# Two heads' scores side by side in the row halves of the array, the decay in one pass, and a gate row made earlier

## The chip, the cores and the metric

The kernel runs on one core of one Trainium2 chip, as one program. The metric is device time in microseconds (us), the median of three runs. A lower number is better. Everything is fp32 in and out. TensorE is the engine PE in the rows, VectorE is DVE, ScalarE is ACT, GpSimd is POOL, SyncE is SP.

## What is computed

One sequence of 512 tokens of width 1024 goes through a first block and then two further layers. The parts that the change touches, in short form:

```
# first block, branch a (sparse attention), 8 heads of 64
dots  = einsum('bqhd,bsd->bqhs', qi, ki)            # 8 index heads, ONE shared key
score = einsum('bqhs,bqh->bqs', relu(dots), wi)     # then causal, top 128 keys per query
logits = (qa . ka) * 64**-0.5, on the kept keys     # 8 heads, ONE shared key
# first block, branch b (forgetting attention), 8 heads, own keys
c = cumsum(log_sigmoid(fb + b_forget))              # per head
logits[t,s] = (qb_t . kb_s) * 64**-0.5 + c_t - c_s, causal
# second layer pair, odd layer: neighbourhood attention, 8 heads, own keys
logits = [ (q . k_window) * 64**-0.5 + bias , (q . k_ctx) * 64**-0.5 ]
# odd layer, fourier branch and the end
y = real(fft2(u)); out = (gates * [attention, y]) @ w_out
x = x + gate_row * rmsnorm(out)                     # gate_row: a modulation of the layer
```

The term c_t is the same for all keys of a query and drops out of the softmax. The kernel adds only minus c_s, called the decay.

## The kernel before, in words

**Number format.** Each fp32 operand of a large product is split in a high part (fp32r) and a low part (the rest, also fp32r), and a product is made of three passes: high times high, high times low, low times high. All passes of a product accumulate in one PSUM bank. A bank holds 128 partitions times 512 columns.

**Weights.** A list `STREAM` orders all weight matrices in units of 128 x 512. ACT makes a unit's high part (L1209), POOL its low part (L1043, `low_weights`), PE consumes it (L591, `tiles`). Four units fit (`ROOM = 4`). `high(u)` makes ACT cast up to unit u, and `ahead(chunk)` casts a chunk and the next three units. ACT works strictly in program order, so a wait ahead of such a cast also holds up the weights.

**Attention as a pipeline by hand.** In three stages PE goes through steps s. A step has the scores of a head for 128 queries (one stationary tile, the keys moving), four transposes or fewer of an older step's probabilities, for every second step the values product, and some pieces of a large matrix product that is fed in between (`feed`). The stages are:

- index stage, 24 steps `("i", i)`, heads outside, query tiles t = 1 to 3 inside; the keys are w = 128 (t+1) wide; ACT applies relu (L1339), DVE accumulates (L1950);
- stage ab: 32 steps of branch a, then 32 of branch b, in pairs of heads, w = 128 (t+1), t = 0 to 3. DVE makes the maximum (L2017 or L2022), ACT the exponential (L1379 or L1388), DVE divides (L2033), PE transposes (`turn_both`, L797), ACT and DVE copy, PE makes the values (`values_both`, L811). Scores lie in banks s % 3;
- stage n: 32 steps, keys 512 (bank s % 2) plus 256 of the context (bank 2); lines L975 to L977 scores, L986 transposes (`turn_near`), L999 values, DVE L2342 to L2363, ACT L1716 to L1736. The probabilities lie in three buffers `N_P`.

**Queries before.** A stationary tile always has 128 rows, though a head has 64 features. In the index stage and branch a, where the key is shared and is stored twice, the tile of one head has the high part in one half of the rows and the low part in the other (`STACKED`): two passes, against the high and the low key. In branch b and stage n two heads share a feature tile; the query of one head is made by a mask that zeroes the other's 64 rows: three passes. The masked pairs are prepared per head by ACT (`prep`) and by DVE or POOL (`low_query`, two POOL instructions each in b and n) into the four places of `QM`.

**Decay before.** Branch b adds three more passes per head (`decay`): a stationary tile of 8 rows, the one-hot of the head, against the high decay, the same against the low decay, and identity times causal mask over the 128 columns of the diagonal.

**The values product** writes the two heads of a pair to partitions 0 to 63 and 64 to 127 of one bank, with stationary tiles of 64 columns (`128*64` in the rows).

**The decay itself** is made early (`CT`, one ACT copy L1304 and one DVE subtraction), at a point where ACT's next work is weight casts.

**After the index stage** DVE has 4 rotations, the low keys of b and 16 rounds of top-8 (`L1987`, `L1990`), then gates, and frees PSUM banks for PE as it goes.

**The end of the kernel.** Order on PE: product `ud`, product `dft`, the fourier mix (L1021, L1022), `gate_rows(1)` (L856, two fp32 products of 512 columns, four instructions), products `oo0` and `oo1`. ACT copies the mix, waits for all low parts, issues two row loads (L1782, L1783), waits for DVE to finish the gate row (`act.wait_ge(sig("row1"), 2)`), issues four loads of x, and only then casts the weights of `oo0` beyond the first. DVE makes the gate row (`modulation`, L2052, L2054) when the two row loads are in.

Of the kernel before, what the change touches and what calls it, by code (L numbers as in the profile page):

```python
# [20 lines left out]
F32 = mybir.dt.float32  # L21
# [5 lines left out]
P = 128  # L27
S = 512
# [55 lines left out]
for _name, _w in (("g_pre", 8), ("npre0", 8), ("npre1", 8), ("bmod0", 24), ("bmod1", 24), ("c", 8),  # L84
                  ("c_ctx", 8), ("conv", 12), ("subln", 1), ("b_forget", 1), ("mask2", 2),
                  ("mask4", 4), ("eps", 1)):
    COL[_name] = (_c, _c + _w)
    _c += _w
# [5 lines left out]
def constants():  # L94
# [36 lines left out]
    sel = np.zeros((P, 2 + 2 * P))  # L131
# [6 lines left out]
def lay_out(a):  # L138
# [58 lines left out]
    i = np.arange(P)  # L197
    put("mask2", (i[:, None] // 64 == np.arange(2)[None, :]).astype(f))
    put("mask4", (i[:, None] // 32 == np.arange(4)[None, :]).astype(f))
# [48 lines left out]
def build(nc, dram, out):  # L248

    with ExitStack() as ctx:  # L250
# [16 lines left out]
        MASKR = sb("mask_r", [P, 2, P], F32R)  # L267
# [6 lines left out]
        SEL = sb("sel_sb", [P, 2 + 2 * P])  # L274
# [3 lines left out]
        CT = nc.alloc_sbuf_tensor_at("decay", [HEADS, 2, S], dtype=F32R, offset=nc.sbuf_base - 8 * S)  # L278
# [6 lines left out]
        AR_COLS = 13088  # L285
# [93 lines left out]
        for name in ("i", *ATT):  # L379
            PREPS[name] = n  # L380
            n += HEADS

        def prep_of(name, head):
            return PREPS[name] + head

        def masked_place(name, p):
            return QM[:, p % 4, 0, :], QM[:, p % 4, 1, :]
# [3 lines left out]
        STACKED = ("i", "a")  # L391
        own_half = lambda head: slice(64 * (head % 2), 64 * (head % 2) + 64)
        other_half = lambda head: slice(64 - 64 * (head % 2), 128 - 64 * (head % 2))

        def place_before(name, p):
            p, first = p - 4, PREPS["n"] if name == "n" else 0
            return p if p >= first else None

# [104 lines left out]
        N_P = arena(6912, 3, S + L)  # L503
# [5 lines left out]
        N_ROW = arena(2048, D)  # L509
        N_BROW, N_NROW = arena(4096, D), arena(5120, D)  # L510
# [9 lines left out]
        IDENT_R, CAUSAL_R = MASKR[:, 0, :], MASKR[:, 1, :]  # L520

        @block.tensor
        def _(pe):
# [197 lines left out]
            def scores(key, bank, name, prep, t, kh, kl, extra=()):  # L721


                pe.wait_ge(sig("qm"), prep + 1)
                qh, ql = masked_place(name, prep)
                c = P * t % qh.shape[-1]
                qh, ql = qh[:, c:c + P], ql[:, c:c + P]
                queries = (qh,) if name in STACKED else (qh, ql)
                n_keys = kh.shape[-1]
                acc = (open_bank if n_keys <= 512 else open_two)(key, bank)  # L730
                for c0 in range(0, n_keys, 512):
                    part = slice(c0, min(c0 + 512, n_keys))
                    passes = [*((q, kh[:, part], c0) for q in queries), (qh, kl[:, part], c0), *extra]
                    for n, (l, r, c) in enumerate(passes):
                        mm = pe.matmul(acc[:, c:c + r.shape[-1]], l, r, start=n == 0, stop=n == len(passes) - 1)
                fills_bank(mm, key)
                qm_last[prep] = key
# [22 lines left out]
            for h in range(HEADS):  # L760
                for t in range(1, ST):
                    i = 3 * h + t - 1
                    w = P * (t + 1)
                    scores(("i", i), i % 4, "i", prep_of("i", h), t, BH[:, 1, 0:w], BL[:, 1, 0:w])
                    feed("i", pieces, n_pieces * (i + 1) // 24 - n_pieces * i // 24)
# [8 lines left out]
            def decay(head, t, w):  # L774
                one = MASKR[0:HEADS, 0, head:head + 1].broadcast_to((HEADS, P))
# [1655 lines left out]
```

## Time and profile before

| what | value |
|---|---|
| median of 3 runs | 1522.4 us (1521.38 to 1523.36) |
| the profiled execution, its own time | 1522.15 us |
| its span, first to last instruction | 1520.4 us |
| mean granted TensorE clock | 0.954 |
| PE busy | 1359.3 us (89%) |
| DVE, ACT, POOL busy | 681.5, 652.5, 474.8 us |

Busy time is summed over the whole span. Matmuls are pipelined, so the recorded durations of neighbours overlap; what one costs is the distance from its start to the start of the next. Where a load of the stationary tile can't be done in advance, the recorded start of the matmul is that of the load.

### The profile page before, as it was taken

To read this page: it belongs to the slowest core of one execution; us is meant where nothing else is said; L and a number is where in the kernel's file an instruction comes from. 1 tells how busy PE (TensorE), PEld (TensorE's weight loads), DVE (VectorE), ACT (ScalarE), POOL (GpSimd) and SP (SyncE) were. 2 spreads that over 40 slices of the span, in tenths; PEclk is the share of its full clock that TensorE was granted. 3 is DMA by queue.
4 is the path that set the end of the run, shared out by engine and by line. 5 is a ranking of instruction groups with operands and counts; after the bars stand their busy time and mean duration, and the time that the engine had idled before them with its cause. 6 is when DMAs were issued, how large, how long until landed. Compare 5 with 4: busy or idle time off the path is not lost. (4 is left out here: it accounts for less than half of the span.)

```text
span 1520.4 us, 20649 instructions
## 1 busy us (share of the span) xinstructions
PE 1359.3 (89%) x7468; PEld 1087.5 (72%) x7468; DVE 681.5 (45%) x1357; ACT 652.5 (43%) x1410; POOL 474.8 (31%) x388
## 2 busy tenths in 40 slices
PE   7999789999999869869999899996795899999986
PEld 6778567877668657658777777786584787888765
DVE  2154982744413332360547756714404612765323
ACT  4435134644352334342346565634224423665423
POOL 3333243432234423313223333322231333421322
PEclk9999899999999989979999999998897999999998
DMA  5122243000242553332152330011213221221331
GB/s 189 67 82 83 83 142 136 29 29 29 80 143 83 190 188 133 112 125 84 56 149 66 85 92 29 29 56 39 110 60 125 99 92 56 81 67 40 139 138 55
DMA packets 27874, 139.40 MB, mean 92 GB/s; under 512 B 4096, under 2 KB 5760, under 8 KB 15232
## 3 DMA queue, kind: packets, MB, share of 16 engines
q1 hardware_dynamic: 20640, 115.42, 22.3%
q10 hardware_dynamic: 7136, 22.67, 4.2%
q8 instruction: 62, 1.02, 0.3%
q14 instruction: 36, 0.29, 0.1%
HBM read 122.35 MB, written 6.29 MB: 85 GB/s over the span
## 5 line engine op out<-in xcount | busy, mean ns | idle before, releaser
L1043 POOL TENSOR_TENSOR w_low<-w_raw,w_high 128x512 fp32r<-128x512 f32 x296 | 386.7, 1317 | 877.4 <-ACT w_high L1209 877.1
L1209 ACT CAST w_high<-w_raw 128x512 fp32r<-128x512 f32 x296 | 178.7, 622 | 509.6 <-PE psum L591 338.4
L591 PE MATMUL psum<-x_high,w_high 128*128 128x512 f32 (+1 forms) x600 | 253.5, 422 | 30.3 <-DVE arena L2282 11.5
L591 PE MATMUL psum<-x_high,w_low 128*128 128x512 f32 (+1 forms) x600 | 238.4, 397 | 0.0
L591 PE MATMUL psum<-x_low,w_high 128*128 128x512 f32 (+1 forms) x600 | 238.2, 397 | 0.0
L591 PEld LDWEIGHTS psum<-x_high,w_high 128*128 128x128 f32 (+1 forms) x600 | 114.5, 191 | 72.1 <-issue 39.0
L591 PE MATMUL psum<-w_high,x_high 128*128 128x512 f32 (+1 forms) x352 | 139.5, 396 | 15.9 <-ACT w_high L1209 7.8
L591 PE MATMUL psum<-w_low,x_high 128*128 128x512 f32 (+1 forms) x352 | 135.4, 385 | 0.0
L591 PE MATMUL psum<-w_high,x_low 128*128 128x512 f32 (+1 forms) x352 | 135.2, 384 | 0.0
L591 PEld LDWEIGHTS psum<-x_high,w_low 128*128 128x128 f32 (+1 forms) x600 | 114.1, 190 | 26.9 <-issue 0.3
L591 PEld LDWEIGHTS psum<-x_low,w_high 128*128 128x128 f32 (+1 forms) x600 | 115.1, 192 | 18.8 <-issue 1.0
L591 PEld LDWEIGHTS psum<-w_high,x_high 128*128 128x128 f32 x352 | 67.3, 191 | 42.6 <-issue 12.4
L2215 DVE TENSOR_REDUCE small<-psum 128x1 f32<-128x768 f32 (+1 forms) x96 | 69.9, 769 | 36.4 <-PE psum L883 36.4
L1556 ACT ACTIVATE arena<-psum,small 128x768 f32<-128x768 f32 (+1 forms) x96 | 72.3, 762 | 17.2 <-DVE small L2215 16.7
L591 PEld LDWEIGHTS psum<-w_low,x_high 128*128 128x128 f32 x352 | 67.5, 192 | 13.4 <-issue 1.0
L591 PEld LDWEIGHTS psum<-w_high,x_low 128*128 128x128 f32 x352 | 67.4, 191 | 13.5
L1088 POOL TENSOR_SCALAR arena<-arena,small 128x768 f32<-128x768 f32 (+1 forms) x48 | 40.5, 843 | 98.4 <-DVE small L2222 98.4
L1565 ACT COPY arena<-psum 128x512 f32<-128x512 f32 (+1 forms) x80 | 36.8, 460 | 76.3 <-PE psum L891 76.1
L2227 DVE SCALAR_TENSOR_TENSOR arena<-arena,small 128x768 f32<-128x768 f32 (+1 forms) x48 | 40.1, 834 | 21.0 <-POOL arena L1088 20.6
L891 PE MATMUL psum<-squares_sb,arena 128*128 128x128 f32 x224 | 38.3, 275 | 8.8 <-DVE arena L2227 8.3
L701 PE MATMUL psum<-squares_sb,arena 128*128 128x128 f32 x96 | 15.7, 320 | 31.9 <-DVE arena L2158 31.9
L619 PE MATMUL psum<-x_high,w_high 128*128 128x512 f32 x96 | 43.1, 449 | 0.0
(312 smaller groups left out, 2718.1 us busy)
## 6 DMA issues: line engine op xcount, KB each, us to landing
w_raw<-stream SPq DMA_DIRECT2D x98, 1024.0 KB, 4.8
x_kept<-arena ACTq DMA_DIRECT2D x8, 512.0 KB, 4.2
arena<-x_kept ACTq DMA_DIRECT2D x8, 512.0 KB, 6.3
arena<-bias ACTq DMA_DIRECT2D x8, 448.0 KB, 3.4
arena<-rows ACTq DMA_DIRECT2D x6, 512.0 KB, 5.2
q_masked<-e_q_high SPq DMA_DIRECT2D x24, 96.0 KB, 2.2
arena<-x SPq DMA_DIRECT2D x4, 512.0 KB, 5.5
arena<-x ACTq DMA_DIRECT2D x4, 512.0 KB, 6.8
```

Of the source, the lines that this page charges most:

```text
L591: mm = pe.matmul(o, l, r, start=(first and n == 0 and kind != "fc"), stop=(last and n == len(passes) - 1))
L619: mm = pe.matmul(o, l, r, start=k == 0 and n == 0, stop=k == NK - 1 and n == 2)
L701: mm = pe.transpose(acc[:, P * t:P * t + P], src[t][:, P * k:P * k + P], ident)
L891: mm = pe.transpose(acc[:, P * (kt - c):P * (kt - c) + P], map_place(s, 0)[:, P * kt:P * kt + P], ident)
L1043: pool.tensor_tensor(WL[:, u % ROOM, :], RAW[:, g % 2, u % 4, :], WH[:, u % ROOM, :].bitcast(F32), ALU.subtract).then_inc(w_lo, 1)
L1088: pool.tensor_scalar(second, second, SM[:, RINV + c + 1:RINV + c + 2], SM[:, 82:83], ALU.mult, ALU.mult)\
L1209: act.copy(WH[:, u % ROOM, :], RAW[:, g % 2, u % 4, :]).then_inc(w_hi, 1)
L1556: frees(act.activation(map_place(s, m), PS[:, 512 * b:512 * b + w], ACT.Exp, bias=scr(NEGMAX + c), accum_out=scr(ROWSUM + c)), key)
L1565: frees(act.copy(E_PT[:, 2 * (d % 2) + hh, P * c:P * c + w], ps[:, 0:w]), key)
L2215: dve.tensor_reduce(scr(NEGMAX + 2 * (s % 4) + m), PS[:, 512 * b:512 * b + w], AX.X, ALU.max, negate=True).then_inc(sig("e_neg"), 1)
L2227: dve.scalar_tensor_tensor(e0, e0, scr(RINV + c), e1, ALU.mult, ALU.add).then_inc(sig("e_p"), 1)
```

## The change

1. **Pairs.** The queries are no longer masked or stacked. ACT casts the whole feature tile of a pair of heads (128 rows) as the high part, and one DVE or POOL instruction makes the low part. The number of preparations halves.
2. **Row halves.** `score_pair` issues for both heads of a pair the three passes with stationary tiles of 64 rows, rows 0 to 63 for the first head and 64 to 127 for the second, alternating, into two banks. It is used in the index stage, in a, b and n.
3. **Decay.** The high decay lies on partitions 0 to 7 and 64 to 71, the low on 32 to 39 and 96 to 103, zeros between. One pass of 40 rows per head replaces two of 8. DVE clears the tile first, ACT copies twice, DVE subtracts twice, and ACT makes a small one-hot tile `HEAD_R`.
4. **Order.** In the stages ab and n the scores of two steps are made at the even step, after the transposes of that step. In n the transposes are split in two groups with half of the fed pieces between them, in one bank; the context scores get banks 2 and 3; the probabilities get a fourth buffer; values come one step later. In the index stage the heads are paired and the sums are taken in the order 0, 2, 1, 3, 4, 5 of each six.
5. **The end.** `gate_rows(1)` stands between `ud` and `dft`. ACT issues the two row loads and the guest copy ahead of the copies of `ud`. DVE makes the gate row right after the low parts of `ud`. ACT casts one more unit ahead of the copies of the mix, and no longer waits for `row1`. The rows lie in other buffers (`N_ROW` in `GROW`, `N_BROW` and `N_NROW` in `MA`).

```diff
+            def score_pair(keys, banks, prep, t, kh, kl, more=()):
+                pe.wait_ge(sig("qm"), prep + 1)
+                qh, ql = (q[:, P * t:P * t + P] for q in query_place(prep))
+                accs = [open_bank(key, bank)[:, 0:kh.shape[-1]] for key, bank in zip(keys, banks)]
+                passes = [(qh, kh), (ql, kh), (qh, kl)]
+                for n, (q, k) in enumerate(passes):
+                    for hh, acc in enumerate(accs):
+                        rows = half_of(hh)
+                        mm = pe.matmul(acc, q[rows, :], k[rows, :], start=n == 0, stop=not more and n == 2)
+                        if not more and n == 2:
+                            fills_bank(mm, keys[hh])
...
-                return ((one, CT[:, 0, 0:w], 0), (one, CT[:, 1, 0:w], 0), (IDENT_R, CAUSAL_R, P * t))
...
+                accs = score_pair(keys, (s % 3, (s + 1) % 3), prep_of(name, pr), t, kh, kl, more=name == "b")
+                if name == "b":
+                    for hh, acc in enumerate(accs):
+                        rows, head = slice(64 * hh, 64 * hh + 40), 2 * pr + hh
+                        pe.matmul(acc, HEAD_R[rows, head:head + 1].broadcast_to((40, P)), CT[rows, 0:w],
+                                  start=False, stop=False)
+                    for hh, acc in enumerate(accs):
+                        fills_bank(pe.matmul(acc[:, P * t:w], IDENT_R, CAUSAL_R, start=False, stop=True), keys[hh])
...
             for s in range(len(BOTH) + 7):
-                if s < len(BOTH):
-                    score_both(s)
                 if 4 <= s < len(BOTH) + 4:
                     turn_both(s - 4)
+                if s < len(BOTH) and s % 2 == 0:
+                    score_both(s)
...
-            for s in range(steps + 3):
-                if s < steps:
-                    score_near(s)
+            for s in range(steps + 4):
                 if 2 <= s < steps + 2:
-                    turn_near(s - 2)
-                if s >= 4 and s % 2 == 0:
-                    values_near((s - 4) // 2)
...
+                    turn_near(s - 2, 0, 4)
+                if s < steps and s % 2 == 0:
+                    score_near(s // 2)
+                if s >= 5 and s % 2:
+                    values_near((s - 5) // 2)
+                n = n_pieces * (s + 1) // n_feeds - n_pieces * s // n_feeds if s < n_feeds else 0
+                feed("n", pieces, n // 2)
+                if 2 <= s < steps + 2:
+                    turn_near(s - 2, 4, 2)
+                feed("n", pieces, n - n // 2)
             pool[0] = ALL
             gemm("ud", X)
+            gate_rows(1)
             gemm("dft", B, ready=turned("ud"))
...
-            gate_rows(1)
             mixed = [(KH[:, k, 0:S], KL[:, k, 0:S]) for k in range(4)] + X[4:]
...
+            def prep(name, pr, q):
+                p = prep_of(name, pr)
                 if place_before(name, p) is not None:
                     filled(act, qm_last[place_before(name, p)])
+                act.copy(query_place(p)[0], q).then_inc(sig("qm_hi"), 1)
...
-            act.copy(CT[:, 0, :], A_F[0:HEADS, 1, :]).then_inc(sig("ct_hi"), 1)
+            for hh in range(2):
+                act.copy(CT[64 * hh:64 * hh + HEADS, :], A_F[0:HEADS, 1, :]).then_inc(sig("ct_hi"), 1)
...
+            act.dma_start(N_BROW, dram["rows"][5:6, :].broadcast_to((P, D))).then_inc(sig("gate_rows1_in"), 16)
+            act.dma_start(N_NROW, dram["rows"][3:4, :].broadcast_to((P, D))).then_inc(sig("gate_rows1_in"), 16)
+            guest_rows("ud")
             for t in range(ST):
                 ps = filled(act, ("ud", t))
                 act.copy(BH[:, t, :], ps[:, :]).then_inc(sig("ud_hi"), 1)
-            guest_rows("ud")
...
+            high(UNITS["oo0"][3])
             for j in range(4):
                 consumed(act, ("fmix", j))
...
-            act.wait_ge(sig("row1"), 2)
...
+            dve.memset(CT[:, :].bitcast(F32), 0.0).then_inc(sig("ct_clear"), 1)
...
+            dve.wait_ge(sig("gate_rows1_in"), 32)
+            modulation(1, (4, 5), (lambda v: N_ROW, N_BROW, N_NROW))
             for i in range(4):
                 dve.wait_ge(sig("gd_sig"), i + 1)
...
-            dve.wait_ge(sig("gate_rows1_in"), 32)
-            modulation(1, (4, 5), (lambda v: N_ROW, N_BROW, N_NROW))
```

## Rows read from the trace of the kernel before

**Rows 1.** The page's first part: busy time, share of the span, instructions.

```profile
PE 1359.3 (89%) x7468; PEld 1087.5 (72%) x7468; DVE 681.5 (45%) x1357; ACT 652.5 (43%) x1410; POOL 474.8 (31%) x388
```

**Rows 2.** Windows: start:end length, busy time (and instructions) of PE, PEld, DVE, ACT, POOL, clock, DMA share, GB/s.

```profile
101.50:156.90 55.40, 54.05 (x240) 45.06 (x241) 25.96 (x32) 27.57 (x53) 20.56 (x16) 0.97 0.23 76
254.89:305.84 50.95, 50.95 (x350) 40.91 (x351) 40.70 (x137) 36.89 (x107) 22.74 (x18) 1.00 0.12 42
305.84:390.92 85.08, 85.08 (x530) 62.11 (x528) 38.82 (x114) 38.49 (x114) 24.46 (x20) 1.00 0.07 26
1279.46:1406.20 126.74, 126.05 (x961) 107.31 (x962) 83.75 (x256) 77.61 (x208) 36.08 (x29) 1.00 0.17 56
1467.30:1474.10 6.80, 6.01 (x14) 4.79 (x15) 0.00 (x0) 1.38 (x3) 4.34 (x4) 0.50 0.90 351
```

**Rows 3.** Timeline of PE, index stage, one head of 384 keys: start, duration, engine, instruction.

```profile
152.03 0.33 PE L735 MATMUL psum<-b_high,q_masked 128*128 128x384 f32 x1
152.21 0.34 PE L735 MATMUL psum<-b_low,q_masked 128*128 128x384 f32 x1
```

**Rows 4.** Timeline of PE, branch b, one head of 512 keys.

```profile
342.73 0.62 PE L735 MATMUL psum<-k_high,q_masked 128*128 128x512 f32 x2
...
343.52 0.72 PE L735 MATMUL psum<-decay,mask_r 8*128 8x512 f32 x2
...
344.35 0.40 PE L797 MATMUL psum<-squares_sb,arena 128*128 128x128 f32 x2
```

**Rows 5.** Timeline of PE, branch b, one head of 128 keys.

```profile
369.66 0.33 PE L735 MATMUL psum<-k_high,q_masked 128*128 128x128 f32 x2
...
370.56 0.51 PE L797 MATMUL psum<-squares_sb,arena 128*128 128x128 f32 x3
```

**Rows 6.** Timeline of PE, stage n: values, fed product, one head's scores, transposes.

```profile
1331.02 1.53 PE L999 MATMUL psum<-arena 128*64 128x128 f32 x24
1332.48 0.50 PE L591 MATMUL psum<-x_high,w_high 128*128 128x512 f32 x1
...
1333.98 0.39 PE L975 MATMUL psum<-k_high,q_masked 128*128 128x512 f32 x1
...
1334.66 0.28 PE L975 MATMUL psum<-k_high,q_masked 128*128 128x256 f32 x1
...
1335.02 0.81 PE L986 MATMUL psum<-squares_sb,arena 128*128 128x128 f32 x6
```

**Rows 7.** Waits in branch b (320 to 391), then stage n (1280 to 1400).

```profile
DVE small L2022 <- PE psum L735: 38.7, 27, 2.4
...
DVE arena L2342 <- PE psum L977: 33.9, 27, 2.2
```

**Rows 8.** Timeline around the decay's making, 43 to 57.5 us.

```profile
47.09 0.48 DVE L1888 MEMSET arena<- 8x512 f32 x1
...
53.68 0.62 ACT L1304 CAST decay<-arena 8x512 fp32r<-8x512 f32 x1 [1.99 <-DVE arena L1903]
...
56.88 0.47 PE L591 MATMUL psum<-x_high,w_high 128*128 128x512 f32 x1 [2.86 <-POOL w_low L1043]
```

**Rows 9.** Timeline of PE after the index stage, its two idle times.

```profile
169.41 0.77 PE L591 MATMUL psum<-x_high,w_high 128*128 128x512 f32 x1 [8.88 <-DVE k_low L1858]
...
228.20 0.79 PE L591 MATMUL psum<-w_high,x_high 128*128 128x512 f32 x1 [5.79 <-DVE gate_b L1977]
```

**Rows 10.** Timeline of the end, 1424 to 1470 us.

```profile
1433.06 0.71 PE L591 MATMUL psum<-w_high,b_high 128*128 128x512 f32 x1 [2.46 <-DVE b_low L1858]
...
1452.56 1.88 PE L856 MATMUL psum<-mod_rows,sel_sb 128*128 128x512 f32 x4
...
1455.96 0.33 ACTq L1782 DMA_DIRECT2D arena<-rows  x1
...
1464.15 1.30 ACTq L1786 DMA_DIRECT2D arena<-x_kept  x3
...
1468.09 0.76 PE L591 MATMUL psum<-w_high,k_high 128*128 128x512 f32 x1 [5.46 <-POOL w_low L1043]
```

More of the change, by code:

```diff
@@ L130, in constants @@
     dft = np.concatenate([np.cos(w[:, 0:S // 2 + 1]), np.sin(w[:, 1:S // 2])], 1)
-    sel = np.zeros((P, 2 + 2 * P))
+    sel = np.zeros((P, 2 + 2 * P + HEADS))
+    for h in range(HEADS):
+        sel[h::32, 2 + 2 * P + h] = 1
     for v in range(2):
@@ L502, in build @@
         N_B = arena(5120, 2, 14 * 64)
-        N_P = arena(6912, 3, S + L)
+        N_P = [arena(6912 + (S + L) * n, S + L) for n in range(3)] + [arena(12288, S + L)]
         N_PT = arena(9216, 4, S + L)
@@ L719, in rotate @@
                     fills_bank(pe.matmul(acc[:, :], square(perm), q, start=True, stop=True), (name, i))
-            def scores(key, bank, name, prep, t, kh, kl, extra=()):
+            def score_pair(keys, banks, prep, t, kh, kl, more=()):
                 pe.wait_ge(sig("qm"), prep + 1)
[L725 to L737, printed above, removed]
+                qh, ql = (q[:, P * t:P * t + P] for q in query_place(prep))
[7 more added lines that the diff above has]
+                            fills_bank(mm, keys[hh])
+                qm_last[prep] = keys[-1]
+                return accs
             pe.wait_ge(sig("ident_in"), 16)
@@ L1094, in _ @@
             low_weights(at, UNITS["n_v"][1])
-            for head in range(2):
-                low_query("n", head)
+            low_query("n", 0)
             low_weights(UNITS["n_v"][2], last)
@@ L1353, in _ @@
                 guest_rows(c)
-            for hh in range(2):
-                preps_a(0, hh)
+            prep_a(0)
             ahead("vb")
@@ L1744, in _ @@
             steps = ATT["n"].steps
-            for s in range(steps + 3):
+            for s in range(steps + 4):
                 for c in ("gn0", "gn1", "gd0", "gd1"):
-                    if ended[c] == ("n", s - 1):
+                    if s and ended[c] in (("n", 2 * s - 2), ("n", 2 * s - 1)):
                         gates_raw(c)
-                if 1 <= s <= len(fed["n"]):
-                    high(fed["n"][s - 1] + ROOM)
+                if s:
+                    high(fed["n"][2 * s - 1] + ROOM)
                 if 2 <= s < steps + 2:
```

267 lines of the change are left out of this document (111 added, 156 removed).

## The prediction

> **What bounds the kernel now.** I read the page first, then the windows of the stages that the change touches, then PE's timeline in one period of each, then the waits of the other engines, last PE's idle times. The page says PE 89% [rows 1], but recorded matmuls overlap, so I count distances between starts. In the windows PE is busy practically all the time in the index stage, in a, in b and in n, at clock 1.00 or 0.97, while DVE needs 40.70 of 50.95 us in a, 38.82 of 85.08 in b and 83.75 of 126.74 in n [rows 2]. In b and n DVE waits for score products: 38.7 and 33.9 us [rows 7]. So in all four stages a PE instruction more or less moves the end one for one. After the index stage PE stands idle twice (8.88 and 5.79 us), both times for DVE's chain that starts with the last index sum [rows 9]; that chain moves with the stage's end, so a longer index stage isn't absorbed there. Two more idle times concern the change: 2.86 us for weights behind the making of the decay [rows 8], and 5.46 us at the end, followed by 6.8 us at clock 0.50 [rows 10, 2].
>
> **Unit prices.** Three passes of 512 columns take 1334.66 - 1333.98 = 0.68, so 0.23 each; three of 256 take 0.36, so 0.12 [rows 6]; 384 take 0.18 [rows 3]. A head of b at 512 keys takes 344.35 - 342.73 = 1.62; its five passes and the mask would be 5 x 0.23 + 0.07 = 1.22 [rows 4]. The remaining 0.40 is the price of going from tiles of 128 rows to tiles of 8 rows and back: 0.20 a way. At 128 keys the head takes 0.90, so its six instructions cost 0.50 without the 0.40, 0.08 each [rows 5]. The trace has no half-row tile. I take the same 0.40 for going in and out of half rows; the bounds are 0 and 0.80 (twice, if each half paid for itself).
>
> **Do two halves run at once?** No row shows it for row halves. The nearest are the column halves of the values product: 24 fp32 instructions of 128 columns in 1332.48 - 1331.02 = 1.46 [rows 6]. An fp32 instruction of 512 columns costs 0.43 (four last 1.88, the last 0.59 of it alone [rows 10]), so 128 columns cost 0.107 and 24 in a row 2.6; two at a time give 1.28 plus the change of tile. They overlap fully, and I take that for row halves as well. The bound on the other side is no overlap.
>
> **The parts.** A block of a pair:
> - *Index stage.* Before, two heads by two passes: 4 slots of the width; after, 3 double slots and 0.40. For 256, 384, 512 keys: +0.28, +0.22, +0.17 = +0.67, four pairs of heads: **+2.7**.
> - *Branch a.* The same with 128 keys too (+0.32): +1.0, four times: **+4.0**. DVE then still has room (80% before).
> - *Branch b.* Before, two heads with 1.62, 1.35, 1.08, 0.90 = 9.9 for the four query tiles. After: 3 double slots, one double slot of decay, two masks of 0.08 and one 0.40, that is 1.48, 1.27, 1.04, 0.88 = 4.7. 5.2 less, four times: **-21.0**. Six passes and two changes of tile fewer per pair: this is the main gain.
> - *Stage n.* Before 2 x 1.04 = 2.08 (a head is 1333.98 to 1335.02 [rows 6]); after 1.04 + 0.40. -0.64, 16 times: **-10.2**.
> - *Order.* Moving transposes ahead of scores puts no tile change in or out: scores fall on even steps, values on odd ones. Cost 0.
> - *Preparations.* Half as many on ACT, DVE and POOL, all beside PE: 0 on the path. The cover is that these engines wait for PE.
> - *Making the decay.* It is on the path: PE waits 2.86 for weights whose cast stands behind ACT's copy of the decay [rows 8]. Added to the chain: DVE clearing 512 columns (0.48, as for 8 partitions), a second ACT copy (0.62) and the one-hot copy of 8 columns (between 0 and 0.62, I take 0.15): **+1.2**. The second DVE subtraction (bound 0.7) lies behind the ACT copy and ahead of rotations that PE needs much later: 0.
> - *The end.* The four gate row instructions (4 x 0.43 = 1.7) leave the stretch ahead of `oo0`. They go into the gap before `dft`, where PE waits 2.46 for the copies of `ud` [rows 10]; they themselves wait for ACT's guest copy, so `dft` starts between 0 and 1.7 later; I take 0.7, since the gap is longer than they are: net -1.0. The row loads, issued near 1431, and the gate row that took from 1455.96 to 1464.15 before, 8.2 us, would be through by 1439, under the `dft` product. Then the idle time: PE has three units of `oo0` ready (36 passes, 8.2) and stops at 1462.5 until 1468.09 because ACT stands in the wait for `row1` and issues four x loads from 1464.15 on [rows 10]. Without that wait ACT issues them (4 x 0.44) at 1456, casts, POOL subtracts (1.3): unit four is ready by about 1459.7, ahead of the 1460.8 at which PE needs it. -5.6. Without the pause the clock should not fall: 6.0 us of work at 0.50 gives back 3.0 [rows 2]. Together **-9.6**.
>
> Sum: 1.2 + 2.7 + 4.0 - 21.0 - 10.2 - 9.6 = -32.9 against the profiled execution's 1522.15, which is 0.25 below the median: 1489.3. I predict 1489.5.
>
> **Weighed against the skill.** The change of tile costs 0.20 a way in the rows of b [rows 4]. The Trainium skill, TensorEngine Tiling (Array Packing), Key Properties, says that changing the tiling mode drains the array; it gives no price, and by this rule the trace agrees; it makes the change lose in the index stage and in a, as summed. On the size of the overlap the values product shows two for one [rows 6]. The Trainium skill, TensorE: Matmul & The Clock Gate, Measured speedup vs the span model, gives 3.07 for four row tiles of 32, where four would be ideal; an estimate from that page makes each double slot 1.3 times as dear, some 12 us on the 40 us of double slots, and the sum 1501. I keep full overlap, since the trace's own nearest case has it.
>
> **Rivals.**
> 1. *No overlap of row halves.* Then the change doesn't do what it says: each half costs a slot. Added: index 6.3 (3 x 0.53 x 4), a 7.3, b 9.7, n 16.6, together 40, and the time is 1529, slower. It decides the sign when over four fifths of the overlap is missing. For it: no row has two row halves. Against it: column halves run at once. 8%.
> 2. *Partial overlap, or loads of stationary tiles laid bare.* If inside a block the tile of the next pass can't be loaded while the same rows stream, each further double slot costs another 0.10 (half of the 0.20). There are 2 x 12, 2 x 16, 3 x 16 and 5 x 16 = 184 of them: +18, 1508. Against it: the two 8-row passes of decay have 0.66 between the first's start and the mask's, that is one load and two streams, not two loads. The mechanism is named in the Trainium skill, TensorE: Matmul & The Clock Gate, The mechanism, where a load overlaps a running matmul only in other row groups. 12%, with all sizes between 1500 and 1510.
> 3. *The other engines' round trip.* With scores in pairs, the bank of head s-2 must be free at step s, two steps later, not three. In b a step is about 2.0 after the change; between the fill of a pair and the next PE has 4.0 - 1.5 = 2.5 of other work; DVE's and ACT's whole work of a step is 38.82/32 + 38.49/32 = 2.4 in series [rows 2]. If that is late by 1 us for the eight widest pairs: +8, 1498. In n the same is 2.6 + 2.4 = 5.0 against 7.3 - 1.4 = 5.9: no wait. In a the banks are freed by DVE's first instruction. 15%.
> 4. *More than summed.* The pause before `dft` shrinks so that the clock doesn't fall there either, and the stages' starts get shorter: -4, 1485. Part of the first case's range.
>
> **How the numbers follow.** The first case, full overlap, 62%: 1484 to 1495. The round trip 15%: 1495 to 1502. Partial overlap 12%: 1500 to 1510. No overlap 8%, above 1515. Better than 1484: 3%. The range 1483 to 1507 leaves out the 3%, the 8% and the top of the third case. What a measurement of this kernel tells from no change is about 0.2%, 3 us. Slower by that: 8% of no overlap and 1% of something unseen; faster 89%; within 0.2% 2%.
>
> **What the profile after would show.** Half-row products in pairs with starts a few ns apart and 0.23 to the next pair; a block of b at 512 keys near 1.5 for both heads, one of n near 1.4; b's window some 21 us shorter, n's 10; the index stage and a 3 to 4 us longer. The idle of 2.86 near 54 us longer by about 1.2. At the end no wait of PE for weights in `oo0`, no `row1` wait of ACT, clock 1.00 there. Wrong would be: second halves that start one slot after the first; ACT or DVE holding banks in b; a pause at the gate row before `dft` longer than 2 us; a clock that falls because half-row tiles load the array less.

## The result and the profile after

The changed kernel takes 1509.25 us (1508.78 to 1509.65, four runs), the kernel before 1521.89 in the same series. The ratio is 0.9916, 95% interval 0.9899 to 0.9933. It is faster by 12.6 us; 32.9 were predicted. The profiled execution took 1509.2, its span is 1507.4, the mean granted clock 0.961. One profiled execution of a later kernel (mask tile moved behind, experiment 4) was disturbed and took 2627.55 us; its time and its trace are left out.

The page of the changed kernel, first part, beside [rows 1]: PE's share did not rise.

```profile
PE 1346.7 (89%) x7492; PEld 1041.9 (69%) x7492; DVE 683.3 (45%) x1355; ACT 642.3 (43%) x1396; POOL 444.7 (30%) x360
```

Windows of the changed kernel, in this order: index stage, a, b, stage n (each from its first score product, b and n to the last values product), the end, and the unchanged middle between b and n. Columns as in [rows 2].

```profile
102.84:154.96 52.12, 51.07 (x246) 37.36 (x246) 23.85 (x25) 21.00 (x43) 19.68 (x15) 1.00 0.23 81
257.84:313.31 55.47, 55.17 (x387) 38.38 (x387) 38.98 (x138) 35.34 (x104) 15.44 (x12) 1.00 0.11 39
313.31:386.45 73.14, 69.48 (x543) 50.62 (x543) 41.98 (x121) 39.83 (x122) 15.41 (x12) 1.00 0.12 41
1269.92:1403.17 133.25, 120.94 (x959) 88.60 (x960) 84.22 (x256) 76.07 (x204) 25.42 (x20) 1.00 0.16 53
...
1403.17:1507.30 104.13, 90.09 (x378) 66.81 (x373) 38.91 (x57) 38.19 (x69) 33.70 (x25) 0.95 0.34 121
386.45:1269.92 883.47, 783.70 (x4211) 628.17 (x4206) 352.57 (x522) 360.48 (x731) 266.46 (x220) 0.95 0.29 97
```

The kernel before, b, stage n, end and middle cut at the same events:

```profile
305.84:399.41 93.57, 90.84 (x578) 66.42 (x577) 43.97 (x124) 42.50 (x125) 25.73 (x21) 0.98 0.10 35
1279.46:1405.88 126.42, 125.73 (x960) 107.16 (x960) 83.75 (x256) 77.61 (x207) 35.79 (x28) 1.00 0.17 56
1405.88:1520.30 114.42, 92.74 (x378) 69.96 (x374) 36.97 (x57) 38.14 (x69) 32.49 (x25) 0.92 0.30 111
399.41:1279.46 880.05, 775.84 (x4210) 629.37 (x4207) 352.14 (x520) 361.34 (x732) 268.89 (x223) 0.95 0.29 97
```

| stretch | before | after | measured | predicted |
|---|---|---|---|---|
| to the start of the last rotation product behind the index stage | 159.94 | 162.57 | +2.6 | +3.9 |
| from there to a | 94.95 | 95.27 | +0.3 | 0 |
| a | 50.96 | 55.46 | +4.5 | +4.0 |
| b, to its last values | 93.57 | 73.15 | -20.4 | -21.0 |
| the unchanged middle | 880.05 | 883.47 | **+3.4** | 0 |
| stage n | 126.41 | 133.25 | **+6.8** | -10.2 |
| the end | 114.42 | 104.15 | -10.3 | -9.6 |
| sum | 1520.3 | 1507.3 | -13.0 | -32.9 |

Of the 19.9 us that are missing stage n has 17.0 and the middle 3.4; the rest cancels. Two stages look better than the change made them: the kernel before ran at a granted clock of 0.97 in the index stage [rows 2] and of 0.98 in b, the changed one at 1.00 in both. By these shares the clock alone gives back about 1.7 us in each, so the work saved in b is nearer 18.7 than 20.4.

Stage n is a sharp measure: three traces with the old order there (the kernel before, the same with its buffers shifted in experiment 4, and experiment 5) have 126.41 to 126.63 us, two with the changed order 133.25 and 133.20. The middle is not: in the kernel of experiment 5, which changes only the end, it is 882.20, 2.2 more than before.

**The row halves do what they should.** PE's timeline of the changed kernel, branch b, one pair at 384 keys: products of 64 rows, of 40 rows, two masks, the next fed product.

```profile
355.14 0.62 PE L733 MATMUL psum<-k_high,q_masked 64*128 64x384 f32 x4
355.60 0.33 PE L733 MATMUL psum<-k_low,q_masked 64*128 64x384 f32 x2
355.77 0.34 PE L792 MATMUL psum<-decay,mask_r 40*128 40x384 f32 x2
356.04 0.44 PE L795 MATMUL psum<-mask_r 128*128 128x128 f32 x2
356.31 0.45 PE L594 MATMUL psum<-x_high,w_high 128*128 128x512 f32 x1
```

Both heads take 356.31 - 355.14 = 1.17; the sum had 1.27. The single records of the same pair (start in us, ns from the start before, line, rows, columns):

```
355.141  201  L733   64  384
355.144    3  L733   64  384
355.422  278  L733   64  384
355.425    3  L733   64  384
355.597  172  L733   64  384
355.600    3  L733   64  384
355.768  168  L792   40  384
355.772    4  L792   40  384
356.040  268  L795  128  128
```

The second half starts 3 to 4 ns after the first, and the next pair of products 168 to 172 ns later, which is one slot of 384 columns. Inside the block going in costs 0.10 (278 ns from the first pair to the second instead of 172), going out another 0.10 (268 to the mask). The rest of the price lies in the neighbours' distances, as it does for the 8-row tiles before, where the distance into the first is 327 ns and out of the last 321, with 228 for a slot. The halves overlap in full, and between tiles of 64 rows no load adds time. The round trip of rival 3 (scores in pairs, so that a bank must come back sooner) shows in b as a single wait of that size; all waits of PE in b together are 3.6 us.

```profile
347.14 0.44 PE L733 MATMUL psum<-k_high,q_masked 64*128 64x128 f32 x4 [1.12 <-ACT arena L1367]
```

**Stage n.** Waits of the changed kernel in the stage's window (us, times, longest). Now PE's loader waits 19.0 us for DVE's normalisation, L2329.

```profile
DVE arena L2316 <- PE psum L733: 26.9, 16, 1.7
...
PEld psum L984 <- DVE arena L2329: 19.0, 20, 1.9
...
PE psum L984 <- DVE arena L2337: 9.8, 16, 1.3
```

The same wait in the kernel before:

```profile
PEld psum L986 <- DVE arena L2355: 0.6, 2, 0.3
```

Timeline of the changed kernel around an even step. L733 scores of a pair, L984 transposes, L2316 maximum, L2326 to L2329 normalisation, L2337 DVE's copy of the second group.

```profile
1324.31 0.73 PE L733 MATMUL psum<-k_high,q_masked 64*128 64x512 f32 x4
...
1325.31 0.69 DVE L2316 CUSTOM_DVE_ANT_0 arena<-psum,arena 128x512 f32<-128x512 f32 x1 [1.70 <-PE psum L733]
...
1326.34 0.38 PE L984 MATMUL psum<-squares_sb,arena 128*128 128x128 f32 x2
...
1326.51 0.15 DVE L2326 TENSOR_TENSOR small<-small 128x1 f32<-128x1 f32 x1
...
1326.90 0.62 DVE L2329 TENSOR_SCALAR arena<-arena,small 128x768 f32<-128x768 f32 x1
...
1327.43 0.42 DVE L2337 COPY arena<-psum 128x256 f32<-128x256 f32 x1
...
1327.96 0.42 PEld L984 LDWEIGHTS psum<-squares_sb,arena 128*128 128x128 f32 x4 [0.97 <-DVE arena L2329]
1327.99 0.63 PE L984 MATMUL psum<-squares_sb,arena 128*128 128x128 f32 x4 [0.57 <-DVE arena L2337]
```

DVE does nothing for 1.70 us ahead of the even head's maximum, because the scores of a pair now come only at the even step and behind the transposes. The odd head's normalisation, whose exponentials are long there, stands behind that maximum in DVE's program. It is done at 1327.52, and the four transposes that need it can't start before. They also need the bank of the second group, which DVE's copy gives back at 1327.85. That wait ends last here, by 0.33 us. The copy stands behind the same maximum and the same normalisation in DVE's program, so both waits come from one order; no run separates them. A pair with its full share of fed products takes 8.11 us here from one period to the next, 7.83 before.

**The early chain and the end.** Changed kernel: the wait that answers to the 2.86 of [rows 8], and the end beside [rows 10].

```profile
57.49 0.76 PE L594 MATMUL psum<-x_high,w_high 128*128 128x512 f32 x1 [3.32 <-POOL w_low L1042]
```

```profile
1425.67 0.33 ACTq L1747 DMA_DIRECT2D merge_a<-rows  x1
...
1428.26 1.88 PE L862 MATMUL psum<-mod_rows,sel_sb 128*128 128x512 f32 x4
1430.67 0.50 PE L594 MATMUL psum<-w_high,b_high 128*128 128x512 f32 x1 [0.53 <-DVE b_low L1824]
```

```profile
1454.00:1463.00 9.00, 9.00 (x40) 7.25 (x39) 0.00 (x0) 2.38 (x4) 5.14 (x4) 1.00 0.56 218
```

The gate row fills the gap ahead of `dft`, of which 0.53 is left, and in the first products of `oo0` PE is busy without a break at clock 1.00.

### The profile page after: what moved, and what is told of

Its sections match the earlier page's. It is cut to its first block and busy times, and to the rows that moved or that the text cites. A ratio compares the mean times of both kernels' runs of the same rounds, so it can differ in the third digit from the quotient of the medians.

```text
span 1507.4 us, 20519 instructions
## 1 busy us (share of the span) xinstructions
PE 1346.7 (89%) x7492; PEld 1041.9 (69%) x7492; DVE 683.3 (45%) x1355; ACT 642.3 (43%) x1396; POOL 444.7 (30%) x360
## 5 line engine op out<-in xcount | busy, mean ns | idle before, releaser
L594 PE MATMUL psum<-x_high,w_high 128*128 128x512 f32 (+1 forms) x600 | 258.3, 430 | 29.4 <-DVE arena L2256 11.5
L594 PEld LDWEIGHTS psum<-x_high,w_high 128*128 128x128 f32 (+1 forms) x600 | 113.9, 190 | 79.4 <-issue 42.2
L2201 DVE SCALAR_TENSOR_TENSOR arena<-arena,small 128x768 f32<-128x768 f32 (+1 forms) x48 | 40.0, 834 | 20.1 <-POOL arena L1071 19.9
L897 PE MATMUL psum<-squares_sb,arena 128*128 128x128 f32 x224 | 38.0, 274 | 8.3 <-DVE arena L2201 7.8
L704 PE MATMUL psum<-squares_sb,arena 128*128 128x128 f32 x96 | 16.2, 329 | 31.8 <-DVE arena L2132 31.8
L984 PE MATMUL psum<-squares_sb,arena 128*128 128x128 f32 x192 | 32.5, 278 | 12.2 <-DVE arena L2337 9.8
```

Source lines behind the costliest of these rows:

```text
L594: mm = pe.matmul(o, l, r, start=(first and n == 0 and kind != "fc"), stop=(last and n == len(passes) - 1))
L704: mm = pe.transpose(acc[:, P * t:P * t + P], src[t][:, P * k:P * k + P], ident)
L897: mm = pe.transpose(acc[:, P * (kt - c):P * (kt - c) + P], map_place(s, 0)[:, P * kt:P * kt + P], ident)
L984: mm = pe.transpose(acc[:, P * kt:P * kt + P], N_P[s % 4][:, P * (c + kt):P * (c + kt) + P], ident)
L2201: dve.scalar_tensor_tensor(e0, e0, scr(RINV + c), e1, ALU.mult, ALU.add).then_inc(sig("e_p"), 1)
```

## The experiments

Each ratio is taken against the kernel before, run on the same chip: 1521.77 us beside the runs of experiment 1 and the first three of experiment 4, 1522.93 beside those of experiments 3, 5 and 6 and the shift by 64 bytes more in experiment 4, 1522.28 beside that of experiment 2 and the last two of experiment 4. Stage times are from the trace, cut as in the table.

**1. Where is the loss in n? The normalisation first.** In DVE's program of stage n the odd head's normalisation goes ahead of the next even head's maximum:

```diff
             for s in range(steps + 2):
+                if s % 2 == 0 and 1 <= s <= steps:
+                    norm_n(s - 1, ATT["n"].tile(s - 1))
                 if s < steps:
                     max_n(s, ATT["n"].tile(s))
-                if 1 <= s <= steps:
+                if s % 2 and s <= steps:
                     norm_n(s - 1, ATT["n"].tile(s - 1))
```

> The changed kernel, with one order changed on DVE in stage n: at even steps the division of the step before stands ahead of the maximum of the new pair. Theory O: in stage n PE waits 0.72 us a pair for the division of an odd head, which stands on DVE behind the maximum of a pair whose scores PE makes later; then these waits go and stage n gets about 12 us shorter: 1497. Rival R: DVE's and ACT's round trip as such is too long for scores in pairs; then the wait moves to the next step and the time stays within 3 us of 1509.

Measured: 1500.99 (1499.94 to 1501.23), ratio 0.9866, interval 0.9844 to 0.9888: 8.3 below the changed kernel. Stage n is 124.62, -8.6, the other stages move by 0.4 at most. In its trace the normalisation runs while DVE used to be idle, and the transposes start as it goes:

```profile
1326.52 0.15 DVE L2326 TENSOR_TENSOR small<-small 128x1 f32<-128x1 f32 x1
...
1326.72 0.42 PEld L984 LDWEIGHTS psum<-squares_sb,arena 128*128 128x128 f32 x4 [0.38 <-issue]
...
1326.91 0.62 DVE L2329 TENSOR_SCALAR arena<-arena,small 128x768 f32<-128x768 f32 x1
...
1328.30 0.69 DVE L2316 CUSTOM_DVE_ANT_0 arena<-psum,arena 128x512 f32<-128x512 f32 x1 [0.78 <-PE psum L733]
```

The transposes at 1326.72 are of the even head. The odd head's normalisation is now at 1326.91, ahead of the maximum at 1328.30.

**2. The same loss from PE's side.** The changed kernel, with the pair's scores ahead of the first group of transposes; DVE's order is as changed.

```diff
             for s in range(steps + 4):
-                if 2 <= s < steps + 2:
-                    turn_near(s - 2, 0, 4)
                 if s < steps and s % 2 == 0:
                     score_near(s // 2)
+                if 2 <= s < steps + 2:
+                    turn_near(s - 2, 0, 4)
```

> The changed kernel (1509.25 us) with one undone order: in stage n PE makes a pair's scores ahead of the first group of transposes of the even step, as in the kernel before; DVE's order is not touched. Theory (the loss in n is DVE's order: it starts the maximum of the even head only when PE has made the scores, behind the transposes, and the odd head's normalisation stands behind it): the scores come 0.55 us earlier, DVE's idle time before the maximum of 1.70 us a pair shrinks by as much, and stage n falls by 16 x 0.5 = 8 us at most, 4 to 8; 1501 to 1505. Rival (the loss is the row halves themselves, their tile changes and their context products, or the one bank for both groups alone): stage n keeps its 133 us within 2, 1507.5 to 1511.

Measured: 1500.14 (1495.94 to 1500.84), ratio 0.9847, interval 0.9823 to 0.9872. Stage n is 124.08, -9.2. DVE's idle time ahead of the maximum is smaller:

```profile
1327.27 0.73 PE L733 MATMUL psum<-k_high,q_masked 64*128 64x512 f32 x4
...
1328.26 0.69 DVE L2316 CUSTOM_DVE_ANT_0 arena<-psum,arena 128x512 f32<-128x512 f32 x1 [1.10 <-PE psum L733]
...
1328.52 0.66 PE L984 MATMUL psum<-squares_sb,arena 128*128 128x128 f32 x4
```

Two different edits, each of which breaks the same chain, give the same 9 us. The row halves, the context's tiles and the one bank were in both, so they are not what costs these. The gain is above the 8 that I had put as the most; by the idle time it can be 16 x (1.70 - 1.10) = 9.6.

**3. The bank of the transposes.** Both groups of a step's transposes use bank 4 in turn. In the kernel of experiment 1 with a 64-byte shift (below) the timeline shows the turn-around:

```profile
1326.83 0.38 PE L984 MATMUL psum<-squares_sb,arena 128*128 128x128 f32 x2
...
1327.32 0.42 DVE L2337 COPY arena<-psum 128x256 f32<-128x256 f32 x1 [0.25 <-PE psum L984]
...
1327.89 0.63 PE L984 MATMUL psum<-squares_sb,arena 128*128 128x128 f32 x4
```

From the second group's start to the next first group are 1.06 us; the two transposes and the one fed piece between them take 0.14 + 0.70 = 0.84. The edit puts both pieces of a step behind the second group:

```diff
                 n = n_pieces * (s + 1) // n_feeds - n_pieces * s // n_feeds if s < n_feeds else 0
-                feed("n", pieces, n // 2)
+                feed("n", pieces, 0)
                 if 2 <= s < steps + 2:
                     turn_near(s - 2, 4, 2)
-                feed("n", pieces, n - n // 2)
+                feed("n", pieces, n)
```

> The kernel with the normalisation first and the 64-byte shift (e4_both, 1498.11 us, stage n 124.6 us), and in stage n all fed pieces of a step behind the second group of transposes, none between the groups; the one bank for both groups stays. Theory (the bank's turn-around: from the start of the second group to the next first group 1.03 us pass while the pieces between take 0.84): with both pieces behind the second group 1.5 us are there, the 0.22 us stall of each of 32 steps goes, stage n falls to about 117 to 119 us, the whole to 1490 to 1492. Rival (DVE's or ACT's total work sets the period of 7.33 us a pair): no change, 1497 to 1499. Second rival (the stall moves ahead of the second group, because the first group's copy on ACT is late): 1496 to 1503.

Measured: 1495.54 (1494.08 to 1499.58), ratio 0.983, interval 0.9809 to 0.985. The interval overlaps that of the kernel it is made from (0.9825 to 0.9871), so the whole time alone does not show a gain. The stage does: 121.59 after 124.62, -3.0, less than the 5.6 to 7.6 expected. Kernels with the order of experiment 1 have 124.45 to 124.62 in three traces. The stage windows of the kernels of experiments 1, 2 and 3, in this order:

```profile
1269.33:1393.95 124.62, 120.64 (x959) 88.62 (x960) 88.65 (x256) 75.50 (x204) 24.98 (x20) 1.00 0.17 57
```

```profile
1270.78:1394.86 124.08, 120.66 (x960) 87.17 (x960) 86.17 (x256) 74.83 (x204) 25.35 (x20) 1.00 0.18 57
```

```profile
1267.56:1389.15 121.59, 114.84 (x960) 91.19 (x960) 80.26 (x256) 75.28 (x204) 27.11 (x19) 1.00 0.16 59
```

In experiment 3 most pairs take 7.12 us (transposes 0.53 + values 1.46 + transposes 0.19 + fed 1.48, then 0.53 + scores 1.25 + 0.19 + 1.49), as good as the 7.19 that the sum has (7.83 less 0.64), though not by its terms: the scores of a pair take 1.25, not 1.44, and the transposes in two groups 0.15 more than before. 16 x 7.12 = 113.9. What is above it sits in a few places: 1.7 us ahead of the first transposes, 2.3 ahead of the second group of the second head, 0.9 near the tail, and 2.0 in three waits behind a values product, one of them in this row, where ACT had a weight cast and two gate copies ahead of the copy:

```profile
1330.62 0.41 PE L984 MATMUL psum<-squares_sb,arena 128*128 128x128 f32 x2 [0.70 <-ACT arena L1708]
```

**4. The middle: is it the place of the buffers?** The change makes the mask tile 8 columns (32 bytes) longer, and all buffers behind it move, the weight buffers first (`w_high` from 108672 to 108704). Six runs vary the place. The kernel before with 32 unused bytes behind the mask tile:

```diff
-        MASKR = sb("mask_r", [P, 2, P], F32R)
+        MASKR = sb("mask_r", [P, 2 * P + HEADS], F32R)[:, 0:2 * P].rearrange("p (a n) -> p a n", a=2)
```

> The kernel before with 8 unused columns behind its tile of identity and mask, so that the weight buffers lie 32 bytes off a multiple of 64, as in the changed kernel. Nothing else differs. Theory A: 227 ns becomes 233 ns throughout and the time rises from 1522 to about 1538 to 1540. Theory B: 1522.

Measured: 1527.08 (1525.43 to 1531.11), ratio 1.0035, interval 1.002 to 1.005: the shift alone costs 5.3 us, a third of what was expected, and its middle is 884.59, +4.5. The distance from one 512-column product to the next did change as expected: its median over all neighbours with 200 to 260 ns between their starts (3053 to 3285 in a trace) goes from 227 to 234 ns, its mean from 228.4 to 233.1. That would be 3285 x 4.7 ns = 15 us. But the median granted clock of these runs is 0.957, and 0.953 beside them, which is worth some 6 us (an estimate, 0.004 x 1522), and where PE waits for another engine a slower product costs nothing. The runs don't separate the two.

The changed kernel, and the kernel of experiment 1, with `w_high` 32 bytes further, at 108736:

```diff
-        MASKR = sb("mask_r", [P, 2 * P + HEADS], F32R)
+        MASKR = sb("mask_r", [P, 2 * P + 2 * HEADS], F32R)
```

> The changed kernel with 8 unused columns (32 bytes) behind the one-hot tile, so that the buffers of weights and everything behind them lie 32 bytes further, at multiples of 64 bytes for the weights as in the kernel before. In the changed kernel two products of 512 columns of any large matrix stand 233 ns apart, before 227, in every part of the program, also where the code is the same. Theory A: the cause is the place of the weight buffers, at 32 beyond a multiple of 64; then the distance falls back to 227 ns and some 3300 products give back 5.5 ns each, about 18 us: 1491. Theory B: the distance has another cause (the profile, the other instructions); then 1509, as the changed kernel.

> Both edits: the 8 columns and the order on DVE. With theories A and O the two add up: about 1479 to 1481. With B and O 1497, with A and R 1491.

Measured: 1507.78 (1504.05 to 1508.35), ratio 0.9907, interval 0.9882 to 0.9932, which can't be told from the changed kernel; and 1498.11 (1496.41 to 1499.25), ratio 0.9848, interval 0.9825 to 0.9871, against 1500.99 without. Both are far from the 1491 and the 1479 to 1481 of theory A. The middle is 886.55 and 883.10. How much of the 3.4 comes back can't be read from this: the two differ by 3.4 themselves, with the same places of buffers, and the granted clock of the middle is 0.944 in the first, 0.948 in the second and 0.950 in the kernel before and the changed one. The spacing is the sharper measure: streams of weights run at 228 to 231 ns in these (means by operand), streams of x still at 233.

The last one with 64 bytes more, `w_high` at 108800, a multiple of 128 as before:

```diff
-        MASKR = sb("mask_r", [P, 2 * P + 2 * HEADS], F32R)
+        MASKR = sb("mask_r", [P, 2 * P + 4 * HEADS], F32R)
```

> e4_both with 32 columns instead of 16 behind the mask tile, so that the weight buffers start at a multiple of 128 bytes as in the kernel before (108800; e4_both has 108736, the changed kernel 108704). Theory (products of 512 columns run at 227 ns when the weight buffers are on a 128-byte boundary, at 233 to 234 when they are not): the spacing goes back to 227 in the stages without attention and 3 to 5 us go, 1493 to 1495. Rival (64 bytes are enough, or it is another buffer whose place matters): within 1 us of e4_both, 1497 to 1499.

Measured: 1501.81 (1499.78 to 1504.78), ratio 0.9868, interval 0.9849 to 0.9888, spacing 232. My theory of the boundary is wrong: 108800 is on a 128-byte and a 256-byte boundary and is no better. Left was the distance to the other operand: `x_high` starts at 1152, 128 past a multiple of 1024, and in the kernel before every large operand does. So the mask tile goes behind the raw weights, which brings `w_high` to 107648, again 128 past; and in a second kernel 32 unused bytes go ahead of everything (the line with `shift`, in that kernel alone; its mask tile has 8 columns less), so that both are 160 past:

```diff
+        sb("shift", [P, 8])
         XH, XL = (sb(n, [P, NK, S], F32R) for n in ("x_high", "x_low"))
...
-        MASKR = sb("mask_r", [P, 2 * P + 2 * HEADS], F32R)
         WH, WL = (sb(n, [P, ROOM, 512], F32R) for n in ("w_high", "w_low"))
         RAW = sb("w_raw", [P, 2, 4, 512])
+        MASKR = sb("mask_r", [P, 2 * P + 2 * HEADS], F32R)
```

> e6_pieces_behind (1495.54 us) with the mask tile behind the raw weights instead of ahead of the weight buffers, so that w_high starts at 107648, the same 128 bytes past a multiple of 1024 as x_high (1152) and all other operand buffers of PE, as in the kernel before; no other edit. e8_aligned_128 has w_high on a 256-byte boundary and ran at 232 ns a product, so the boundary alone is not what counts. Theory (the distance between the buffer of the loaded tile and that of the streamed one counts, and must be a multiple of 1024, or 256 or more): spacing 227 ns again as in the kernel before, 5 to 6 us less, 1489 to 1491. Rival (the place of the arena or of the small buffers counts, which stay shifted): spacing 229 to 233, 1494 to 1497.

> e9_mask_behind with 32 unused bytes ahead of all buffers: x_high at 1184, w_high at 107680, both at 160 past a multiple of 1024. Theory of the distance: 227 ns as e9, within 1 us of it. Rival theory of the boundary (a buffer 32 bytes off a 64-byte boundary is read more slowly, whatever the other one): 233 ns, 5 to 6 us more than e9.

Measured: 1489.72 (1486.61 to 1491.47, three executions and no trace, ratio 0.9781, interval 0.9753 to 0.981) and 1490.79 (1489.78 to 1491.49, ratio 0.9789, interval 0.9765 to 0.9814), 5.8 and 4.8 us below experiment 3, on which both are built (the intervals of the ratios touch it, 0.9809 against 0.981 and 0.9814). Six products of 512 columns at the same place of the program, in the kernel before, the changed kernel and the second of these two:

```profile
62.45 0.39 PE L591 MATMUL psum<-x_high,w_low 128*128 128x512 f32 x1
...
63.81 0.39 PE L591 MATMUL psum<-x_high,w_low 128*128 128x512 f32 x1
```

```profile
62.27 0.40 PE L594 MATMUL psum<-x_high,w_low 128*128 128x512 f32 x1
...
63.67 0.40 PE L594 MATMUL psum<-x_high,w_low 128*128 128x512 f32 x1
```

```profile
62.48 0.39 PE L595 MATMUL psum<-x_high,w_low 128*128 128x512 f32 x1
...
63.84 0.39 PE L595 MATMUL psum<-x_high,w_low 128*128 128x512 f32 x1
```

1.36, 1.40 and 1.36 for six: 227, 233 and 227 ns. Over the whole trace the last kernel has a median of 227 and a mean of 228.2, as the kernel before. The distance decides, not the boundary. The stages of the last kernel gain over experiment 3 by 0.9 (index), 1.6 (to a), 1.3 (middle) and 0.6 (end), while n is 1.3 longer, 2.6 in the span. The middle is 881.43, 1.4 above that of the kernel before, which is less than the 2.2 that the kernel of experiment 5 has above it with no buffer moved.

**5. The end alone.** The kernel before with part 5 of the change and nothing else.

```diff
             gemm("ud", X)
+            gate_rows(1)
             gemm("dft", B, ready=turned("ud"))
...
-            gate_rows(1)
...
             act.wait_ge(sig("nix_lo"), 8)
...
-            act.wait_ge(sig("row1"), 2)
```

The two row loads and DVE's gate row stand where part 5 puts them.

> The kernel before with the fifth part of the change alone: gate_rows(1) between ud and dft, the row loads ahead of the copies of ud, the gate row right behind the low parts of ud, one more unit cast ahead of the copies of the mix, no wait for row1. Theory: the end is worth what the prediction says and does not need the rest; the whole kernel gets 9.5 to 10.5 us shorter, all of it after the last values product of stage n (114.4 us before, 104.1 in the changed kernel). Rival (the gain at the end stands on the shift of a whole stage, for example on raw weights that have landed earlier): less than 7 us.

Measured: 1511.67 (1510.65 to 1511.92), ratio 0.993, interval 0.9915 to 0.9945, -11.3, a little more than expected; the end is 102.49 us long, -11.9. It needs nothing of the rest.

**6. The shared-key stages as before.** Experiment 3's kernel with the index stage and a in two passes of 128 rows. A pair has two planes of `QM`; the plane of a head holds its high part in its own half and its low part in the other.

```diff
+            def score_stacked(keys, banks, prep, t, kh, kl):
+                pe.wait_ge(sig("qm"), prep + 1)
+                for hh in range(2):
+                    acc = open_bank(keys[hh], banks[hh])[:, 0:kh.shape[-1]]
+                    q = query_place(prep)[hh][:, P * t:P * t + P]
+                    pe.matmul(acc, q, kh, start=True, stop=False)
+                    fills_bank(pe.matmul(acc, q, kl, start=False, stop=True), keys[hh])
+                qm_last[prep] = keys[-1]
...
```

> e6_pieces_behind with the shared-key stages as before: in the index stage and branch a a stationary tile of 128 rows holds a head's high part in its own half and the low part in the other, two passes a head instead of three in row halves, and no change of tile shape; b and n keep the pairs in row halves. Theory: branch a falls from 55.4 to 51.0 us, the index stage by 1 to 2 us, together 5 to 6.5 us less than e6_pieces_behind. Rival (the pairing of the steps, not the third pass, costs the time in a): less than 1 us.

Measured: 1494.94 (1492.74 to 1498.13), ratio 0.9824, interval 0.9802 to 0.9846: no measurable difference from experiment 3. Branch a is 52.12 long, -3.3, and the index stage with its rotations 0.7 shorter, so the third pass and the tile change did cost what is theirs; four products of 256 columns now make 273.59 - 273.04 = 0.55.

```profile
273.04 0.36 PE L733 MATMUL psum<-b_high,q_masked 128*128 128x256 f32 x1
273.24 0.28 PE L734 MATMUL psum<-b_low,q_masked 128*128 128x256 f32 x1
273.36 0.28 PE L733 MATMUL psum<-b_high,q_masked 128*128 128x256 f32 x1
273.47 0.28 PE L734 MATMUL psum<-b_low,q_masked 128*128 128x256 f32 x1
273.59 0.39 PE L598 MATMUL psum<-x_high,w_high 128*128 128x512 f32 x1
```

But a begins 2.1 us later after the rotations, and the index stage 1.8 later. The first may come from the double preparation, two instructions each on ACT and POOL, but the kernel before with the 32-byte shift has 97.4 us there too, 2.5 more than without; the second is within what this start varies by between kernels (100.4 to 104.3). Neither was tested.

## Why the prediction was wrong

- *PE sets the time.* Right in a, b and the index stage. In n right for the kernel before, and wrong for the changed one: there the clear sign is PE's 19.0 us wait for DVE.
- *Unit prices, tile change 0.20 a way.* Right to 0.1 us for the block in b: 1.17 against 1.27 at 384 keys. In n the block takes 1.25 against 1.44; the transposes beside it take back 0.15 of that.
- *Full overlap.* Right: 3 ns between the halves. Rivals 1 and 2 are out. So is the estimate of 1501 from the Trainium skill (TensorE: Matmul & The Clock Gate, Measured speedup vs the span model): its 3.07 is for four row tiles, and the two row tiles here overlap in full.
- *Index +2.7, a +4.0, b -21.0, decay +1.2.* Measured: index and early chain together +2.6 instead of +3.9, a +4.5, b -20.4. In this the index stage by itself has +1.3 (159.94 - 101.52 = 58.42 before, 162.57 - 102.84 = 59.73 after) and would have +3.0 at one clock; that its sum and that of b came out so close is in part the clock's doing, so luck. The wait behind the decay grew from 2.86 to 3.32 and its end moved from 56.88 to 57.49, half of the 1.2 that I gave it.
- *Order: cost 0.* **This is the step that failed**, with "in n 5.0 against 5.9: no wait" of rival 3 (by the prediction's own sum a period is 7.1 after the change, not 7.3, so it should read 5.7). It asked only whether a tile change comes in, and compared sums of work. What the moved order changes is when DVE gets its scores and what stands behind them in its program: the odd head's normalisation behind a maximum that waits 1.70 us. Experiments 1 and 2 give this 8.6 and 9.2 us, half of the 17.0. The split of the groups into one bank, which I counted at nothing as part of the same step, has at least 3.0 (experiment 3). That leaves 5.4 of the 17.0. The waits listed in experiment 3 add up to 6.9, and the kernel before, whose waits of PE inside the stage are 0.7, has little of that kind; so they are large enough to hold all 5.4. They were read, not tried.
- *Rival 3 in b.* It cost one wait of 1.12 us, and all waits of PE there 3.6, not 8.
- *Stage n -10.2.* The saving of PE work is real (a pair of 7.12 in experiment 3); in the changed kernel the waits took it.
- *The end -9.6.* Right: -10.3, and -11.9 alone. Of the pause of up to 1.7 ahead of `dft` 0.53 is idle time. Without the pause for weights the clock stays at 1.00, as summed.
- *What I did not count at all.* A buffer that grows by 32 bytes. It costs 5.3 us in the kernel before; putting the buffers back at the old distance gives 4.8 by the medians and 2.6 by the spans. The middle's +3.4 is likely part of it; how much stays open, since the middle was 2.2 longer in a kernel that moves no buffer.

The best kernel here, pairs in row halves in all stages, normalisation first, pieces behind, buffers at the old distance, takes 1489.7 to 1490.8. That is what the prediction had for the change as it stands, but it takes three edits that the prediction did not have.

## What to carry to other kernels

When producer instructions are batched (the scores of two heads at once), write down for every consumer engine its program order with the time at which each operand is ready: what stands behind the first wait is late too, however much idle time the engine has. Give each reused bank its turn-around time, from the first write to the give-back, and compare it with the work between. And after any change of a buffer's size, compare the spacing of products in a stage that was not touched.

## What the runs showed of the hardware

- The spacing of 512-column products depends on where the streamed and the loaded operand lie relative to each other. With buffers whose start addresses are equal modulo 1024 its median is 227 ns and its mean 228 (both 128 past, or both 160 past); with a difference of 32 bytes the mean is 233, of 128 bytes 232, of 64 bytes 228 to 231 where weights stream and 233 where x does. That is 2% on PE's main work. No other equal distance was tried, so the period may be less than 1024. Why, the traces don't tell.
- Two tiles of 64 rows start 3 to 4 ns apart and stream at full pace, and the next tile is loaded into each half while that half streams: 168 to 172 ns a double slot of 384 columns.
- The change between tiles of 128 and of 64 rows adds 0.10 us to the distance behind the first tile and 0.10 to that behind the last, at 384 keys. Going to 8 rows and back adds the same 0.10 (327 and 321 ns for 228) to the distances ahead of the first and behind the last.
